# Attention stage of a hybrid decoder layer: turning the values inside the steps

## The chip, the cores and the metric

The kernel runs on one core of a Trainium2 chip. The metric is the device time of one execution in microseconds (us), as the median of three runs. Beside it stands one execution recorded by the hardware profiler, from which all rows below come.

## The reference

One layer: RMS norm, one wide input projection, three token mixers (a chunked state-space scan, a dilated sliding-window attention, a short gated convolution), each projected and merged with gates, an output projection, a norm and the residual. The change is in the attention. For each of 8 heads and three patterns (window, dilation) = (128, 1), (512, 4), (2048, 16), a query looks at 128 earlier keys that lie `dilation` apart, and at itself:

```
def dilated_window_attention(q, k, v, window, dilation):
    ...
    kb = key_blocks(k)
    vb = key_blocks(v)
    ...
    scores = jnp.einsum("brnqhd,brnkhd->brnhqk", qb, kb) * (ATTN_HEAD_DIM ** -0.5)
    scores = jnp.where(valid[None, None, :, None], scores, -jnp.inf)
    m = jnp.max(scores, axis=-1, keepdims=True)
    p = jnp.exp(scores - m)
    den = jnp.sum(p, axis=-1)
    o = jnp.einsum("brnhqk,brnkhd->brnqhd", p, vb) / jnp.moveaxis(den, -1, -2)[..., None]
```

The sequence has 2048 positions, a head has 64 channels, and all is float32. Keys and values are shared by the three patterns; each pattern has its own queries.

## The kernel before, in words

The kernel runs five stages one after the other: projection, scan with gates, attention, merge of the branches, output. `attention_stage` (from line 961) is a program for each engine inside one block, and each engine's program has a loop over four pairs of heads (`PAIRS`, slots 0 and 1 of a pair). Nothing orders the engines but semaphores, and each engine and each DMA queue works in the order written.

The values of a pair come from memory with the channels on the partitions (`v_t`, in the trace a_v) and are needed with the positions on the partitions (`v_tok`, a_vt). TensorE turns them, 12 quarters (`NV`), four for each pattern g, each quarter four transposes of 128 x 128 (L1137) into one of four buffers of `ps_t` (a_pst). VectorE copies the even turns out (L1037), ScalarE the odd ones (L1196, the line of its copy). Before the change all 12 quarters stand at the head of the loop over the pairs, ahead of the first score.

Then come 48 steps (`NS`), index j: slot 0 with patterns 0, 1 and 2, eight steps each (`SPAN`), then slot 1 likewise. A step treats two blocks of 128 queries. Its parts:

- score(j), TensorE, L1155: queries against the high and the low part of the keys (`k_hi`, `k_lo`; strided by the dilation), into `ps_s`. It waits for mask j-2.
- mask, VectorE, L1238: scale, mask and row maximum.
- exp(j), ScalarE, L1207.
- turn(j-2), TensorE, L1165: transposes the probabilities into `ps_t`; the evacuation (L1026 to L1030 on VectorE, L1196 on ScalarE) copies them to `probs_t`. The turns of values and of probabilities share one numbering n, by which the buffer (n % 4) and the copying engine (n % 2) are chosen; before, n is 12 + j for the probabilities.
- output(j-4), TensorE, L1179: probabilities times values, 65 columns; VectorE copies four blocks at a time to `att` (L1249).

The keys of a slot are loaded raw by SP (`load_k`, L1060, two loads of 512 KB), split by ScalarE (`split_hi`, L1047) and POOL (`split_lo`, L1051). ScalarE does the split for slot 1 at j = 10 and the one for the next pair's slot 0 at j = 34, between exp(j) and the copy that belongs to step j.

SP's order within a pair (from L1090) is: wait until `v_turned` says that this pair's 12 quarters are turned, load the next pair's values (L1092), load the keys of slot 1 (L1060), the three queries of slot 1 (L1066), the keys of the next pair, its queries and the stores of `att` (L1075, L1080):

```
sp.wait_ge(v_turned, NV * i + NV)
sp.dma_start(v_t[:], d["kv"][bass.ds(4 + following, 1)].rearrange("o p t -> p (o t)")
             ).then_inc(v_loaded, 16)
load_k(i, 1, 2 * i + 1)
```

Of the kernel before, what the change touches and what calls it, by code (L numbers as in the profile page):

```python
# [21 lines left out]
P = 128  # L22
# [5 lines left out]
HEADS, HDIM, GROUPS, STATE = 16, 64, 4, 128  # L28
# [6 lines left out]
OUT_W = HDIM + 1  # L35
# [925 lines left out]
def attention_stage(nc, w, d, ident, raw, y_lo):  # L961
# [11 lines left out]
    blocks = [[(r, n) for r in range(x) for n in range(SEQ // x // P)] for x in dil]  # L973
    steps = [(g, sl, b) for sl in range(2) for g in range(3) for b in range(0, NB, 2)]
    NS, NV = len(steps), 12
    SPAN = NB // 2
    TURNS = (NS + NV) // 2
    stores = [1, dil[1], 1]
    with ExitStack() as stack:
        s = Scope(nc, stack)  # L980
        q_s = s.sb("a_q", [P, 3, SEQ], F32R)
        k_raw, v_t = s.sb("a_kraw", [P, SEQ]), s.sb("a_v", [P, SEQ])
# [30 lines left out]
        def strided(ap, g):  # L1013
            return ap.rearrange("p (m r) -> p r m", r=dil[g])
# [4 lines left out]
        def evacuate(eng, parity, copy, i, j):  # L1019

            eng.wait_ge(p_turned, NS * i + j + 5)
            eng.wait_ge(o_made, NS * i + j + 1)
            n = NV + j
            g, sl, b = steps[j]
            if width(g, b) == width(g, b + 1) == 2 * P:
                copy(probs_t[:, j % 4], ps_t[:, n % 4]).then_inc(t_taken[parity], 1)  # L1026
            elif width(g, b + 1) == P:
                copy(probs_t[:, j % 4, 1::2], ps_t[:, n % 4, 1::2]).then_inc(t_taken[parity], 1)
            else:
                copy(probs_t[:, j % 4, 1:], ps_t[:, n % 4, 1:]).then_inc(t_taken[parity], 1)  # L1030

        def evacuate_v(eng, parity, copy, i):

            eng.wait_ge(o_made, NS * i + 4)
            for n in range(parity, NV, 2):
                eng.wait_ge(v_turned, NV * i + n + 1)
                copy(v_tok[:, n // 4, n % 4 * 4:n % 4 * 4 + 4].rearrange("p b (s q) -> p b s q", q=OUT_W)[:, :, :, :HDIM],  # L1037
                     ps_t[:, n % 4].rearrange("p b (s q) -> p b s q", q=HDIM)).then_inc(t_taken[parity], 1)

        def scored(unit, g):  # L1040

# [2 lines left out]
        def split_hi(act, unit, sl):  # L1044
            act.wait_ge(k_loaded, 32 * unit + 32)
            act.wait_ge(s_made, NS + NS // 2 * (unit - 1))
            act.activation(k_hi[:, sl], k_raw[:], ACT.Copy).then_inc(k_hi_made, 1)  # L1047
# [5 lines left out]
        with nc.Block() as block:  # L1053
# [70 lines left out]
            @block.tensor  # L1124
            def _(pe):
                pe.sem_inc(s_made, NS)
                pe.sem_inc(p_turned, 4)
                pe.sem_inc(o_made, 4)
                pe.wait_ge(ones_made, 1)
                with pe.Fori(0, PAIRS) as i:  # L1130
                    pe.wait_ge(v_loaded, 16 * i + 16)
                    for n in range(NV):
                        g = n // 4
                        pe.wait_ge(t_taken[n % 2], TURNS * i + n // 2 + 1)
                        for b in range(4):
                            r, m = blocks[g][n % 4 * 4 + b]
                            last = pe.transpose(ps_t[:, n % 4, b], strided(v_t[:], g)[:, r, m * P:(m + 1) * P], ident[:])  # L1137
                        last.then_inc(v_turned, 1)

                    def score(j):  # L1140
                        g, sl, b = steps[j]
                        if b == 0:
                            pe.wait_ge(q_loaded[g], 32 * i + 16 * sl + 16)
                            if g == 0:
                                pe.wait_ge(k_made, 2 * i + sl + 2)
                        pe.wait_ge(masked, NS * i + j + 1)
                        bank = ps_s[:, j % 2].rearrange("p e k -> p (e k)")
                        for e in range(2):

                            at = (b + e) * P  # L1150
                            r, m = blocks[g][b + e]
                            n = width(g, b + e)
                            for k, first in ((k_hi, True), (k_lo, False)):
                                keys = strided(k[:, sl], g)[:, r, (m + 1) * P - n:(m + 1) * P]
                                last = pe.matmul(bank[:, (e + 1) * 2 * P - n:(e + 1) * 2 * P], q_s[:, g, at:at + P], keys,  # L1155
                                                 start=first, stop=not first)
                        last.then_inc(s_made, 1)

                    def turn(j):
                        g, sl, b = steps[j]  # L1160
                        pe.wait_ge(exped, NS * i + j + 5)
                        pe.wait_ge(t_taken[j % 2], TURNS * i + (NV + j) // 2 + 1)
                        for e in range(2):
                            for h in range(2 - width(g, b + e) // P, 2):
                                last = pe.transpose(ps_t[:, (NV + j) % 4, 2 * e + h], probs[:, j % 4, e, h * P:(h + 1) * P],  # L1165
                                                    ident[:])
                        last.then_inc(p_turned, 1)

                    def output(j):
                        g, sl, b = steps[j]  # L1170
                        if j == 0:
                            pe.wait_ge(t_taken[1], TURNS * i + NV // 2 + 2)
                        pe.wait_ge(t_taken[j % 2], TURNS * i + (NV + j) // 2 + 3)
                        if j % 2 == 0:
                            pe.wait_ge(o_taken, 24 * i + j // 2 + 1)
                        for e in range(2):
                            first = 2 - width(g, b + e) // P
                            for h in range(first, 2):
                                last = pe.matmul(ps_o[:, j // 2 % 2, (b + e) % 4, :OUT_W], probs_t[:, j % 4, 2 * e + h],  # L1179
                                                 v_tok[:, g, b + e - 1 + h, sl * OUT_W:(sl + 1) * OUT_W],  # L1180
                                                 start=h == first, stop=h == 1)
                        last.then_inc(o_made, 1)

                    for j in range(NS + 4):
                        if j < NS:
                            score(j)
                        if 2 <= j < NS + 2:
                            turn(j - 2)
                        if j >= 4:
                            output(j - 4)  # L1190

            @block.scalar
            def _(act):
                act.sem_inc(exped, 4)
                act.sem_inc(t_taken[1], 2)
                copy = lambda to, of: act.activation(to, of, ACT.Copy)  # L1196
                split_hi(act, 0, 0)
                with act.Fori(0, PAIRS) as i:
                    evacuate_v(act, 1, copy, i)
                    for j in range(NS + 2):  # L1200
                        if j < NS:
                            g, sl, b = steps[j]
                            act.wait_ge(masked, NS * i + j + 3)
                            act.wait_ge(p_turned, NS * i + j + 1)
                            for e in range(2):
                                n = width(g, b + e)
                                last = act.activation(probs[:, j % 4, e, 2 * P - n:], scores[:, j % 4, e, 2 * P - n:],  # L1207
                                                      ACT.Exp, bias=att[:, g, b + e, 2 * OUT_W + sl:2 * OUT_W + sl + 1],
                                                      scale=-1.0)
                            last.then_inc(exped, 1)  # L1210

                            if j % (NS // 2) == SPAN + 2:
                                sl = j // (NS // 2)
                                split_hi(act, 2 * i + sl + 1, 1 - sl)
                        if j >= 2 and j % 2:
                            evacuate(act, 1, copy, i, j - 2)

            @block.vector
            def _(dve):
# [4 lines left out]
                    dve.sem_inc(stored[g], 16 * stores[g])  # L1224
                dve.wait_ge(band_turn, 3)
                keys = band[:].rearrange("p a k -> p (a k)")
                with dve.Fori(0, PAIRS) as i:
                    evacuate_v(dve, 0, dve.tensor_copy, i)
                    for j in range(NS + 5):
                        if j < NS:  # L1230
                            g, sl, b = steps[j]
# [8 lines left out]
                                    in1=keys[:, 2 * P - n:], scale=-HDIM ** -0.5, scalar=-NEG, op0=ALU.add, op1=ALU.min,  # L1240
                                    accum_out=att[:, g, b + e, 2 * OUT_W + sl:2 * OUT_W + sl + 1])
                            last.then_inc(masked, 1)
                        if 2 <= j < NS + 2 and j % 2 == 0:
                            evacuate(dve, 0, dve.tensor_copy, i, j - 2)
                        if j >= 6 and j % 2 == 0:
                            grp = j // 2 - 3
# [639 lines left out]
```

## Time and profile before

| | us |
|---|---|
| median of three runs | 3264.48 (3257.29 to 3268.20) |
| profiled execution, own time | 3256.7 |
| its span, first to last instruction | 3255.0 |
| TensorE busy | 3087.3 (95%) |
| VectorE, ScalarE, POOL busy | 1072.2, 859.7, 750.5 |
| attention stage, first transpose to last output | 2257.2 to 2628.6 |

The page of the profile gives the busy time of each engine as a share of the span; the trace itself can be asked for stretches, for what each engine waited for, and for the instructions in order of time. PE is TensorE, PEld its weight loads, DVE VectorE, ACT ScalarE, SP the engine that issues loads. A name such as `a_pst<-ident,a_v` is the tile written and the tiles read. "[6.34 <-DVE a_vt L1037]" is idle time before an instruction and what ended it; "issue" stands where the profile shows nothing that was waited for.

### The profile page before, as it was taken

To read this page: it belongs to the slowest core of one execution; us is meant where nothing else is said; L and a number is where in the kernel's file an instruction comes from. 1 tells how busy PE (TensorE), PEld (TensorE's weight loads), DVE (VectorE), ACT (ScalarE), POOL (GpSimd) and SP (SyncE) were. 2 spreads that over 40 slices of the span, in tenths; PEclk is the share of its full clock that TensorE was granted. 3 is DMA by queue.
4 is the path that set the end of the run, shared out by engine and by line. 5 is a ranking of instruction groups with operands and counts; after the bars stand their busy time and mean duration, and the time that the engine had idled before them with its cause. 6 is when DMAs were issued, how large, how long until landed. Compare 5 with 4: busy or idle time off the path is not lost. (4 is left out here: it accounts for less than half of the span.)

```text
span 3255.0 us, 42118 instructions
## 1 busy us (share of the span) xinstructions
PE 3087.3 (95%) x15420; PEld 2598.0 (80%) x15420; DVE 1072.2 (33%) x1821; ACT 859.7 (26%) x1459; POOL 750.5 (23%) x406
## 2 busy tenths in 40 slices
PE   6999999999999999999999999998899968989798
PEld 5888888888888888888887888887898856778687
DVE  6003434201000011110002544544565567762333
ACT  5110000000000000000113455554566642332232
POOL 7111111111111111112233353451111034421000
PEclk9999999999999999999999999999999989999999
DMA  5121222334421210112324344444544457775543
GB/s 156 61 74 64 75 73 77 87 113 129 116 71 64 77 35 23 39 39 92 97 91 130 106 129 111 117 132 163 149 121 139 143 179 234 237 243 143 173 137 116
DMA packets 333307, 370.78 MB, mean 114 GB/s; under 512 B 22832, under 2 KB 283952, under 8 KB 319664
## 3 DMA queue, kind: packets, MB, share of 16 engines
q1 hardware_dynamic: 314864, 270.51, 28.7%
q10 hardware_dynamic: 16080, 91.23, 8.1%
q0 software_dynamic: 2304, 8.39, 0.7%
q8 instruction: 20, 0.33, 0.0%
q14 instruction: 39, 0.32, 0.0%
HBM read 234.43 MB, written 135.66 MB: 114 GB/s over the span
## 5 line engine op out<-in xcount | busy, mean ns | idle before, releaser
L281 PE MATMUL p_acc<-h,w_hi 128*128 128x512 f32 x2464 | 968.9, 393 | 3.5 <-DVE h L482 3.4
L283 PE MATMUL p_acc<-h,w_lo 128*128 128x512 f32 x2464 | 964.7, 392 | 0.0
L282 PE MATMUL p_acc<-h,w_hi 128*128 128x512 f32 x2464 | 958.8, 389 | 0.0
L283 PEld LDWEIGHTS p_acc<-h,w_lo 128*128 128x128 f32 x2464 | 462.7, 188 | 104.5
L282 PEld LDWEIGHTS p_acc<-h,w_hi 128*128 128x128 f32 x2464 | 462.9, 188 | 101.3
L281 PEld LDWEIGHTS p_acc<-h,w_hi 128*128 128x128 f32 x2464 | 463.1, 188 | 99.8 <-DVE h L482 4.8
L242 POOL CAST w_hi<-raw 128x1024 fp32r<-128x1024 f32 x88 | 91.6, 1041 | 1349.9 <-PE p_acc L283 1344.5
L1556 PE MATMUL b_acc<-b_yhi,b_whi 128*128 128x512 f32 x512 | 206.0, 402 | 44.5 <-DVE b_ylo_ssd L1647 26.5
L244 POOL TENSOR_TENSOR w_lo<-raw,w_hi 128x1024 fp32r<-128x1024 f32 x88 | 212.1, 2410 | 7.0
L379 ACT ACTIVATE p_stage<-p_acc 128x1024 f32<-128x1024 f32 (+1 forms) x45 | 64.2, 1427 | 554.0 <-PE p_acc L283 554.0
L1558 PE MATMUL b_acc<-b_yhi,b_wlo 128*128 128x512 f32 x512 | 203.1, 397 | 0.0
L1207 ACT ACTIVATE a_probs<-a_scores,a_att 128x256 f32<-128x256 f32 (+1 forms) x384 | 155.6, 454 | 101.2 <-DVE a_att L1238 99.0
L509 DVE TENSOR_SCALAR work<-p_acc,p_cw,p_cb 128x2048 f32<-128x2048 f32 x16 | 38.6, 2410 | 383.9 <-PE p_acc L283 383.9
L1238 DVE CUSTOM_DVE_ANT_0 a_scores<-a_pss,a_band 128x256 f32<-128x256 f32 (+1 forms) x384 | 125.1, 363 | 115.9 <-PE a_pss L1155 113.4
L765 PE MATMUL s_acc<-h,w_hi 128*128 128x512 f32 x384 | 162.5, 423 | 0.0
L1179 PE MATMUL a_pso<-a_vt,a_probst 128*128 128x65 f32 x1200 | 156.1, 269 | 0.0
L1556 PEld LDWEIGHTS b_acc<-b_yhi,b_whi 128*128 128x128 f32 x512 | 98.7, 193 | 70.3 <-issue 36.1
L767 PE MATMUL s_acc<-h,w_lo 128*128 128x512 f32 x384 | 150.4, 392 | 0.0
L1179 PEld LDWEIGHTS a_pso<-a_vt,a_probst 128*128 128x128 f32 x1200 | 149.8, 193 | 0.3
L766 PE MATMUL s_acc<-h,w_hi 128*128 128x512 f32 x384 | 149.7, 390 | 0.0
L535 DVE TENSOR_TENSOR work<-p_acc,work 128x2048 f32<-128x2048 f32 x4 | 9.2, 2293 | 417.4 <-PE p_acc L283 417.4
L1432 POOL TENSOR_TENSOR b_wlo<-b_raw,b_whi 128x2048 fp32r<-128x2048 f32 (+2 forms) x20 | 82.1, 4103 | 231.1 <-ACT b_whi L1466 231.1
(196 smaller groups left out, 4208.2 us busy)
## 6 DMA issues: line engine op xcount, KB each, us to landing
raw<-w_in SPq DMA_DIRECT2D x113, 512.0 KB, 4.2
a_q<-s_qs SPq DMA_DIRECT2D x27, 1024.0 KB, 5.7
b_gate<-s_gates SPq DMA_DIRECT2D x48, 512.0 KB, 7.1
s_xbc<-p_stage ACTq DMA_DIRECT2D x16, 1024.0 KB, 3.9
work<-s_xbc SPq DMA_DIRECT2D x16, 1024.0 KB, 6.9
b_att<-s_att SPq DMA_DIRECT2D x24, 528.0 KB, 5.7
s_qs<-p_stage ACTq DMA_DIRECT2D x24, 512.0 KB, 5.5
s_qs<-work ACTq DMA_DIRECT2D x24, 512.0 KB, 8.2
```

The costliest lines, as they stand in the source:

```text
L244: pool.tensor_tensor(w_lo[:, slot], raw[:, slot], w_hi[:, slot], ALU.subtract).then_inc(w_made[slot], 1)
L281: pe.matmul(to, w_hi[:, slot, c], h_hi, start=c == 0, stop=False)
L282: pe.matmul(to, w_hi[:, slot, c], h_lo, start=False, stop=False)
L283: last = pe.matmul(to, w_lo[:, slot, c], h_hi, start=False, stop=c == KC - 1)
L765: pe.matmul(acc_tiled, w_hi[:, slot, b], hi, start=b == 0, stop=False)
L766: pe.matmul(acc_tiled, w_hi[:, slot, b], lo, start=False, stop=False)
L767: last = pe.matmul(acc_tiled, w_lo[:, slot, b], hi, start=False, stop=b == KC - 1)
L1179: last = pe.matmul(ps_o[:, j // 2 % 2, (b + e) % 4, :OUT_W], probs_t[:, j % 4, 2 * e + h], v_tok[:, g, b + e - 1 + h, sl * OUT_W:(sl + 1) ...
L1207: last = act.activation(probs[:, j % 4, e, 2 * P - n:], scores[:, j % 4, e, 2 * P - n:], ACT.Exp, bias=att[:, g, b + e, 2 * OUT_W + sl:2 * ...
L1238: last = dve.tensor_tensor_reduce(out=scores[:, j % 4, e, 2 * P - n:], in0=ps_s[:, j % 2, e, 2 * P - n:], in1=keys[:, 2 * P - n:], scale=- ...
L1556: pe.matmul(to, w_hi[:, k, c], y_hi[:, c, span], start=c == at, stop=False)
L1558: last = pe.matmul(to, w_lo[:, k, c], y_hi[:, c, span], start=False, stop=c == at + n - 1)
```

## The change

Each pair now turns its own patterns 1 and 2 and the next pair's pattern 0 within its steps: the quarters of pattern 1 at steps 0 to 3, of pattern 2 at steps 8 to 11, and of pattern 0, from the values of the next pair, at steps 36 to 39. In each of these steps TensorE turns the quarter between score(j) and turn(j-2). Pair 0's pattern 0 is turned ahead of the loop; the last pair turns four quarters that nobody uses. The numbering of turns is now made from a list of both kinds in order (`turns`, `turn_of`), starting at 4. The engine that copies a probability turn follows from it and is another one for steps 0 to 9. Waits are added so that the outputs of a pattern come after its values, and values are overwritten only when the outputs that read them are done. SP's program has not been edited.

```diff
+    FIRST = NV // 3
...
+    v_at = {at + n: (g, n) for g, at in ((1, 0), (2, SPAN), (0, 4 * SPAN + 4)) for n in range(NV // 3)}
+    turns = [x for j in range(NS + 4) for x in ([("v", *v_at[j])] if j in v_at else []) + (
+        [("p", j - 2)] if 2 <= j < NS + 2 else [])]
+    turn_of = {x: FIRST + n for n, x in enumerate(turns)}
...
+        def evacuate_v(eng, parity, copy, i, j):
+
+            g, quarter = v_at[j]
+            done = FIRST + list(v_at).index(j) + 1
+            eng.wait_ge(o_made, NS * i + {0: 4 * SPAN + 4, 1: 1, 2: 4}[g])
+            eng.wait_ge(v_turned, NV * i + done)
+            take_v(parity, copy, g, quarter, turn_of["v", g, quarter])
...
+                pe.wait_ge(v_loaded, 16)
+                for n in range(FIRST):
+                    pe.wait_ge(t_taken[n % 2], n // 2 + 1)
+                    turn_values(0, n, n)
                 with pe.Fori(0, PAIRS) as i:
-                    pe.wait_ge(v_loaded, 16 * i + 16)
-                    for n in range(NV):
-                        g = n // 4
+                    def turn_v(j):
+                        g, quarter = v_at[j]
+                        n = turn_of["v", g, quarter]
+                        if g == 0 and quarter == 0:
+                            pe.wait_ge(v_loaded, 16 * i + 32)
                         pe.wait_ge(t_taken[n % 2], TURNS * i + n // 2 + 1)
...
                     def output(j):
                         g, sl, b = steps[j]
+                        n = turn_of["p", j]
+                        if sl == 0 and b == 0 and g > 0:
+                            for quarter in (2, 3):
+                                v = turn_of["v", g, quarter]
+                                pe.wait_ge(t_taken[v % 2], TURNS * i + v // 2 + 3)
...
                         if j < NS:
                             score(j)
+                        if j in v_at:
+                            turn_v(j)
                         if 2 <= j < NS + 2:
                             turn(j - 2)
...
                 split_hi(act, 0, 0)
+                evacuate_first_v(act, 1, copy)
                 with act.Fori(0, PAIRS) as i:
-                    evacuate_v(act, 1, copy, i)
...
-                        if j >= 2 and j % 2:
+                        if j in v_at and turn_of["v", *v_at[j]] % 2:
+                            evacuate_v(act, 1, copy, i, j)
+                        if j >= 2 and turn_of["p", j - 2] % 2:
                             evacuate(act, 1, copy, i, j - 2)
...
+                evacuate_first_v(dve, 0, dve.tensor_copy)
                 with dve.Fori(0, PAIRS) as i:
-                    evacuate_v(dve, 0, dve.tensor_copy, i)
...
-                        if 2 <= j < NS + 2 and j % 2 == 0:
+                        if j in v_at and turn_of["v", *v_at[j]] % 2 == 0:
+                            evacuate_v(dve, 0, dve.tensor_copy, i, j)
+                        if 2 <= j < NS + 2 and turn_of["p", j - 2] % 2 == 0:
                             evacuate(dve, 0, dve.tensor_copy, i, j - 2)
```

## Rows read from the trace of the kernel before

**Rows 1.** The page: busy us and share of the span of each engine.

```profile
PE 3087.3 (95%) x15420; PEld 2598.0 (80%) x15420; DVE 1072.2 (33%) x1821; ACT 859.7 (26%) x1459; POOL 750.5 (23%) x406
```

**Rows 2.** Stretch of pair 1: us; busy PE, PEld, DVE, ACT, POOL; PEclk, DMA, GB/s.

```profile
2365.00:2443.00 78.00, 77.07 (x637) 74.69 (x635) 50.19 (x239) 52.46 (x123) 9.11 (x2) 1.00 0.45 133
```

**Rows 3.** Timeline from pair 0 to pair 1 (start, duration, engine, line, what).

```profile
2351.43 1.92 PE L1137 MATMUL a_pst<-ident,a_v 128*128 128x128 f32 x16
2351.70 1.28 ACT L1196 ACT_TABLE_LOAD   x1 [1.07 <-PE a_pso L1179]
2352.23 0.71 SPq L1080 DMA_DIRECT2D s_att<-a_att  x1
...
2358.94 1.29 DVE L1037 COPY a_vt<-a_pst 128x512 f32<-128x512 f32 x2 [6.88 <-issue]
2359.69 5.56 PE L1137 MATMUL a_pst<-ident,a_v 128*128 128x128 f32 x32 [6.34 <-DVE a_vt L1037]
...
2365.01 0.31 PE L1155 MATMUL a_pss<-a_khi,a_q 128*128 128x128 f32 x1
2365.51 0.37 SPq L1092 DMA_DIRECT2D a_v<-s_kv  x1
2365.91 0.29 DVE L1238 CUSTOM_DVE_ANT_0 a_scores<-a_pss,a_band 128x128 f32<-128x128 f32 x1 [0.39 <-PE a_pss L1155]
2366.18 1.18 SPq L1060 DMA_DIRECT2D a_kraw<-s_kv  x2
```

**Rows 4.** Waits of the attention stage (who for whom: total us, times, longest).

```profile
DVE a_vt L1037 <- issue: 20.1, 3, 6.9
```

**Rows 5.** Timeline, head of pair 0.

```profile
2256.67 4.52 POOL L1051 TENSOR_TENSOR a_klo<-a_kraw,a_khi 128x2048 fp32r<-128x2048 f32 x1 [8.20 <-ACT a_khi L1047]
2257.17 7.54 PE L1137 MATMUL a_pst<-ident,a_v 128*128 128x128 f32 x48 [14.76 <-DMA a_v<-s_kv]
...
2264.47 0.31 PE L1155 MATMUL a_pss<-a_khi,a_q 128*128 128x128 f32 x1
...
2265.36 0.29 DVE L1238 CUSTOM_DVE_ANT_0 a_scores<-a_pss,a_band 128x128 f32<-128x128 f32 x1 [0.37 <-PE a_pss L1155]
```

**Rows 6.** Timeline, first steps of pair 1: exp(0) to exp(2), output(0), score(6).

```profile
2366.67 2.59 ACT L1207 ACTIVATE a_probs<-a_scores,a_att 128x128 f32<-128x128 f32 x6 [0.79 <-DVE a_att L1238]
...
2369.88 0.78 PE L1179 MATMUL a_pso<-a_vt,a_probst 128*128 128x65 f32 x6
...
2372.28 0.36 PE L1155 MATMUL a_pss<-a_khi,a_q 128*128 128x256 f32 x1
```

**Rows 7.** Groups by line, attention stage: ScalarE's copy of a value quarter.

```profile
L1196 ACT ACTIVATE a_vt<-a_pst 128x512 f32<-128x512 f32 x24 | 14.0, 597 | 31.5 <-PE a_pst L1137 31.5
```

**Rows 8.** Timeline and one stretch, pair 0, steps 10 to 13: split of keys, turn(11).

```profile
2289.08 1.91 ACT L1047 ACTIVATE a_khi<-a_kraw 128x2048 fp32r<-128x2048 f32 x1 [6.88 <-DMA a_kraw<-s_kv]
...
2291.84 1.12 PE L1165 MATMUL a_pst<-ident,a_probs 128*128 128x128 f32 x4 [5.25 <-ACT a_probs L1207]
```

```profile
2294.00:2296.00 2.00, 2.00 (x11) 1.99 (x11) 0.27 (x3) 0.24 (x1) 1.60 (x1) 0.50 0.04 8
```

**Rows 9.** Timeline, pair 1: score(11), split, turn(9), output(7); then pair 1's end.

```profile
2382.05 0.46 PE L1155 MATMUL a_pss<-a_khi,a_q 128*128 128x256 f32 x1
...
2382.64 1.90 ACT L1047 ACTIVATE a_khi<-a_kraw 128x2048 fp32r<-128x2048 f32 x1
...
2383.02 0.62 PE L1165 MATMUL a_pst<-ident,a_probs 128*128 128x128 f32 x4
...
2383.48 1.00 PE L1179 MATMUL a_pso<-a_vt,a_probst 128*128 128x65 f32 x8
...
2443.97 1.92 PE L1137 MATMUL a_pst<-ident,a_v 128*128 128x128 f32 x16
```

**Rows 10.** Key loads L1060, from issue to landing: pair 1, then pair 0.

```profile
DMA to landing us min/median/max: 7.3/8.2/9.0
...
DMA to landing us min/median/max: 12.7/13.6/14.6
```

More of the change, by code:

```diff
@@ L1022, in evacuate @@
             eng.wait_ge(o_made, NS * i + j + 1)
-            n = NV + j
+            n = turn_of["p", j]
             g, sl, b = steps[j]
@@ L1030, in evacuate, with take_v, evacuate_first_v @@
                 copy(probs_t[:, j % 4, 1:], ps_t[:, n % 4, 1:]).then_inc(t_taken[parity], 1)
[L1032 to L1038, printed above, removed]
+        def take_v(parity, copy, g, quarter, n):
+            copy(v_tok[:, g, quarter * 4:quarter * 4 + 4].rearrange("p b (s q) -> p b s q", q=OUT_W)[:, :, :, :HDIM],
+                 ps_t[:, n % 4].rearrange("p b (s q) -> p b s q", q=HDIM)).then_inc(t_taken[parity], 1)
+        def evacuate_first_v(eng, parity, copy):
+            for n in range(parity, FIRST, 2):
+                eng.wait_ge(v_turned, n + 1)
+                take_v(parity, copy, 0, n, n)
+        def evacuate_v(eng, parity, copy, i, j):
[4 more added lines that the diff above has]
+            take_v(parity, copy, g, quarter, turn_of["v", g, quarter])
         def scored(unit, g):
@@ L1129, in _, with turn_values @@
                 pe.wait_ge(ones_made, 1)
-                with pe.Fori(0, PAIRS) as i:
-                    pe.wait_ge(v_loaded, 16 * i + 16)
-                    for n in range(NV):
-                        g = n // 4
+                def turn_values(g, quarter, n):
+                    for b in range(4):
+                        r, m = blocks[g][quarter * 4 + b]
+                        last = pe.transpose(ps_t[:, n % 4, b], strided(v_t[:], g)[:, r, m * P:(m + 1) * P], ident[:])
+                    last.then_inc(v_turned, 1)
+                pe.wait_ge(v_loaded, 16)
+                for n in range(FIRST):
+                    pe.wait_ge(t_taken[n % 2], n // 2 + 1)
+                    turn_values(0, n, n)
+                with pe.Fori(0, PAIRS) as i:
+                    def turn_v(j):
[3 more added lines that the diff above has]
+                            pe.wait_ge(v_loaded, 16 * i + 32)
                         pe.wait_ge(t_taken[n % 2], TURNS * i + n // 2 + 1)
[L1135 to L1138, printed above, removed]
+                        turn_values(g, quarter, n)
                     def score(j):
@@ L1160, in turn @@
                         g, sl, b = steps[j]
+                        n = turn_of["p", j]
                         pe.wait_ge(exped, NS * i + j + 5)
-                        pe.wait_ge(t_taken[j % 2], TURNS * i + (NV + j) // 2 + 1)
+                        pe.wait_ge(t_taken[n % 2], TURNS * i + n // 2 + 1)
                         for e in range(2):
                             for h in range(2 - width(g, b + e) // P, 2):
-                                last = pe.transpose(ps_t[:, (NV + j) % 4, 2 * e + h], probs[:, j % 4, e, h * P:(h + 1) * P],
+                                last = pe.transpose(ps_t[:, n % 4, 2 * e + h], probs[:, j % 4, e, h * P:(h + 1) * P],
                                                     ident[:])
@@ L1170, in output @@
                         g, sl, b = steps[j]
+                        n = turn_of["p", j]
+                        if sl == 0 and b == 0 and g > 0:
+                            for quarter in (2, 3):
+                                v = turn_of["v", g, quarter]
+                                pe.wait_ge(t_taken[v % 2], TURNS * i + v // 2 + 3)
                         if j == 0:
-                            pe.wait_ge(t_taken[1], TURNS * i + NV // 2 + 2)
-                        pe.wait_ge(t_taken[j % 2], TURNS * i + (NV + j) // 2 + 3)
+                            for quarter in (2, 3):
+                                v = turn_of["v", 0, quarter] - len(turns)
+                                pe.wait_ge(t_taken[v % 2], TURNS * i + max(v // 2 + 3, 4))
+                        pe.wait_ge(t_taken[n % 2], TURNS * i + n // 2 + 3)
                         if j % 2 == 0:
```

## The prediction

> **What bounds the kernel now.** I read the busy shares of the page, then the table of stretches, then the timeline of the attention stage and its waits. TensorE is busy 95% of the span [rows 1], and within a pair of the attention stage 77.07 of 78 us at clock 1.00 [rows 2]: the 48 steps of a pair are bound by TensorE's own stream, and anything put into them costs its full length. Between two pairs it is different. Behind the last output of pair 0 TensorE turns four quarters of the values (16 transposes from 2351.43, 1.92 us), then is idle 6.34 us until VectorE takes the first of them, and turns the other eight in 5.56 us; score(0) starts at 2365.01 and the first mask at 2365.91 [rows 3]. VectorE's own idle time there is not a wait for TensorE: it is charged to "issue", 3 times, 20.1 us in all [rows 4], once at each return to the top of the loop over the pairs. The chain that counts is therefore the one through VectorE's return, 6.88 us of idle time and then the values, before any score can be masked.
>
> **Part 1, between pairs.** After the change the first VectorE work of a pair is mask(0), not a copy of values, and score(0) and score(1) need no VectorE at all. If VectorE still comes back at 2358.94, mask(0) starts there and not at 2365.91: 6.97 us earlier [rows 3]. There are three such places: -20.9 us. The quarters of pattern 1 at steps 0 and 1 lie under VectorE's idle time and cost nothing; without that cover they would cost 0.46 us each.
>
> What does the return cost? The row shows idle time and no cause. The Trainium skill ("Runtime: NRT & Kernel Launch", Instruction fetch mechanics) states that a taken branch whose target lies outside the small fetched window stops the engine until the target page has come by DMA. By that rule the 6.88 us stay whatever work comes first in the loop, which is what the sum above has; were they bound to the value copies they would go too (rival 2). ScalarE and TensorE start their first work of the new pair within about a microsecond, ScalarE at 2351.70 [rows 3], which the rule alone does not explain.
>
> **Part 2, head of pair 0.** All twelve quarters run ahead of score(0) now, 2257.17 to 2264.47, mask(0) at 2265.36. With four quarters left there, the key's low half becomes the last to arrive: it starts at 2256.67 and takes 4.52 us, 2261.19 [rows 5]. Score(0) follows, the mask 0.9 us later as now: 2262.1, or -3.3 us.
>
> **Part 3, refilling the steps.** From mask(0) the chain to the first output takes 3.97 us now and score(6) starts at 6.37 us [rows 3, 6]. ScalarE gets more in it: the table load, now done at 2351.70 ahead of the value copies [rows 3] while nobody waits, comes in front of the first Exp, because that is the first activation of the loop's body (1.28 us); one value copy of 0.60 us [rows 7]; and the turned probabilities of step 0, which VectorE copies now, because the numbering of turns shifts (0.6 us, taken from the same row). ScalarE is thereby 2.5 us late. TensorE has no slack left for the two quarters at steps 2 and 3, and starts from the lower clock after its idle time. Counted from the start of mask(0), ScalarE's order is: mask done 0.8, table 2.1, exp(0) 2.9, exp(1) 3.8 (six Exps take 2.59 us [rows 6], so a step 0.9), value copy 4.4, exp(2) 5.3, copy of probabilities 0 5.9, exp(3) 6.8, copy 1 7.4. Output(0) can start at 5.9, output(1) at 7.4, and with 1.0 us for it score(6) at 8.4: 2.0 later than now. With the lower clock, at which turns and outputs take about twice as long, as behind the idle time in [rows 8], it comes at about 10: 3.6 later. I take 3.0: four pairs, +12 us (8 to 14.4).
>
> The Trainium skill ("ScalarE activation tables: per-element evaluation and per-set limits", Table sets in the compiler and the runtime) says that the table loads are placed block by block. By it the load goes in front of the first Exp in the body; were it placed ahead of the loop, this term would be about 5 us smaller in all. The row has it inside the loop.
>
> **Part 4, quarters inside full steps.** Eight quarters a pair go into steps 8 to 11 and 36 to 39. Four transposes take TensorE from 2383.02 to 2383.48, 0.46 us [rows 9]. 8 x 0.46 = 3.7 us a pair, on the bound itself: +14.7 us. VectorE and ScalarE have room for the copies. In all, 52 quarters are turned instead of 48.
>
> **Part 5, the queue of loads.** This decides. SP waits for all twelve turns of the pair before it reloads a_v, and behind that a_v load in the same queue stand the two loads of the keys of the second slot. Now the twelfth turn comes before step 0. Afterwards it is the turn in step 11. ScalarE, however, asks for these keys in step 10 (split_hi), ahead of the copy of turned probabilities 8 and of exp(11). There is no deadlock, since TensorE reaches turn 11 without them, but then everything stops.
>
> Time from t, the start of score(11). Turn 11 starts at t+0.97 (2382.05 to 2383.02 [rows 9]) and ends at t+1.6. SP issues a_v 0.26 us after the last transpose (2359.69+5.56 to 2365.51), the first key load 0.67 us later and the second 0.6 after that [rows 3]: t+3.2. The second lands 9.0 us after issue [rows 10]: t+12.2. The split takes 1.90 [rows 9], then ScalarE copies probabilities 8, 0.6: t+14.7. Only then output(8) can start. TensorE would have been there at t+2.7 (step 11 with its quarter) plus a score and a turn, 1.4: t+4.1. It idles 10.6 us.
>
> The profile already holds this stall, once. In pair 0 the key loads are issued into a full queue and land after 14.6 us [rows 10]; ScalarE waits 6.88 us for them, TensorE is idle 5.25 us, and works on at granted clock 0.50 [rows 8]. What it costs: pair 0 runs 2264.47 to 2351.43, 86.96 us, pair 1 runs 2365.01 to 2443.97, 78.96 us [rows 3, 5, 9]: 8.0 us, idle 5.25 plus 2.75 for the lower clock (1.2 instead of 2.4 GHz) and the restart. In the same way the new stall costs 10.6 + 2.75 = 13.3 us in each of four pairs, and replaces the one of pair 0: 4 x 13.3 - 8.0 = +45.2 us. Bounds: 12 us a pair if the restart is cheaper (+40), 15.5 if it is dearer (+54), and 5.6 us more if pair 0 lands as late as it does now (14.6 for 9.0).
>
> The query loads behind it in the queue are wanted from step 24 on, more than 20 us later; a_v for the next pair at step 36. Neither is late.
>
> **Sum.** -20.9 - 3.3 + 12 + 14.7 + 45.2 = +47.7 us. On the profiled execution (3256.7 us, span 3255.0) this is 3304; the median of the timed runs, 3264.5, lies 7.8 above it and gives 3312. I take 3310.
>
> **Rivals.**
> 1. The keys are not late, so the stall is missing: the queue would have to let them past a_v, or turn 12 be counted earlier. It decides from a landing at t+1.6 (t+4.1 less 0.6 and 1.90); they would have to land 10.6 us earlier than worked out. Then pair 0's stall goes as well: -20.9 - 3.3 + 12 + 14.7 - 8.0 = -5.5, 3259, no difference that can be told. For it: the first keys in each pair are never waited for in pairs 1 to 3, where the split starts without idle time [rows 9]. Against it: the order in SP's queue and the counts, which are fixed. 5%.
> 2. VectorE's idle time at the loop's top goes with the value copies. Then 3 x 6.6 us or so more are gained: 47.7 - 20 = +28, 3292. For it: ScalarE and TensorE show no such stop. Against it: it is charged to no engine and no DMA, and the work before and after the branch is unchanged in kind, as is the store issued at 2352.23, beside which it falls [rows 3]. The skill's rule on fetching, above, speaks against this rival too. 8%.
> 3. The stall is there and much dearer: the lower clock holds through the following steps, or the key loads meet other traffic in every pair and land after 14.6 us, 5.6 more each: +70, 3334. Against it: in pairs 1 to 3 they land within 9.0. 5%.
> 4. Both 1 and 2: -25, 3239. 2%.
>
> **How the numbers follow.** Forecast 80%, rivals 5, 8, 5 and 2. The forecast's own bounds: below, 3256.7 - 24.2 + 8 + 14.7 + 40 = 3295; above, 3264.5 - 24.2 + 14.4 + 14.7 + 54 + 5.6 = 3329. The range takes in rival 2's time: 3290 to 3328. A measurement of this kernel tells 0.3%, some 10 us. Slower by more than that: forecast and rivals 2 and 3, 93%; within it: rival 1, 5%; faster: rival 4, 2%.
>
> **What would show it.** ScalarE idle before the split of the keys about 11 us in each pair, released by the key load, four times; a_v issued some 30 us after the pair's first score and not 0.5; TensorE idle some 10 us once a pair, in step 12, with clock 0.50 behind it. Between pairs TensorE ahead by two scores and two quarters, VectorE still idle 6 to 7 us, then mask(0) directly; the table load in front of the first Exp. From the score(0) of pair 0 to that of pair 1, 100.5 us now with a stall of its own [rows 3, 5], it becomes about 105.5, and the same in the pairs behind it. The forecast is wrong if ScalarE's wait is short, or if the stop of VectorE is gone.

## The result, and the profile after

The changed kernel takes 3325.4 us (median; 3305.4 to 3334.4), the kernel before 3265.8 us: ratio 1.0175, interval 1.0129 to 1.0222, slower by 1.75%. Each is the median of four executions. The profiled execution takes 3305.4 us (span 3303.7) against 3256.7, so 48.7 us more. The runs of the changed kernel lie further apart than those of the kernel before; the reason is a finding of its own, below.

The waits of the attention stage after the change (who for whom: total us, times, longest):

```profile
ACT a_khi L1064 <- DMA a_kraw<-s_kv: 47.0, 4, 11.9
PEld a_pso L1213 <- issue: 43.3, 4, 11.0
PE a_pso L1213 <- ACT a_probst L1232: 42.3, 4, 10.8
DVE a_scores L1276 <- issue: 21.9, 3, 7.5
```

ScalarE waits for the keys of slot 1 four times, 11.75 us on average, and TensorE four times for ScalarE's copy of the turned probabilities, 42.3 us in all. VectorE's idle time at the loop's return is still there, 21.9 us for 20.1 [rows 4].

The timeline of one such stall, in pair 1 (the answer to [rows 8, 9]):

```profile
2388.69 0.37 SPq L1109 DMA_DIRECT2D a_v<-s_kv  x1
...
2389.36 1.18 SPq L1077 DMA_DIRECT2D a_kraw<-s_kv  x2
...
2398.59 1.91 ACT L1064 ACTIVATE a_khi<-a_kraw 128x2048 fp32r<-128x2048 f32 x1 [11.52 <-DMA a_kraw<-s_kv]
2400.41 0.47 ACT L1232 ACTIVATE a_probst<-a_pst 128x384 f32<-128x384 f32 x1
...
2401.11 1.54 PE L1213 MATMUL a_pso<-a_vt,a_probst 128*128 128x65 f32 x6 [10.35 <-ACT a_probst L1232]
```

SP issues a_v at the twelfth turn, 30.5 us after the pair's first score, and not 0.5 us after it as in [rows 3]; the keys land behind it, are split, and the small copy at 2400.41 releases output(8).

The return from pair 0 to pair 1 (the answer to [rows 3]):

```profile
2358.18 0.32 PE L1181 MATMUL a_pss<-a_khi,a_q 128*128 128x128 f32 x1
...
2359.72 0.65 PE L1150 MATMUL a_pst<-ident,a_v 128*128 128x128 f32 x4
2366.21 0.29 DVE L1276 CUSTOM_DVE_ANT_0 a_scores<-a_pss,a_band 128x128 f32<-128x128 f32 x1 [7.38 <-issue]
...
2366.95 1.28 ACT L1243 ACT_TABLE_LOAD   x1 [9.55 <-DVE a_att L1276]
...
2375.70 0.36 PE L1181 MATMUL a_pss<-a_khi,a_q 128*128 128x256 f32 x1
```

TensorE is two scores and two quarters ahead when VectorE comes back, mask(0) is its first work, the table load stands in front of the first Exp, and score(6) starts at 2375.70.

### The profile page after: what moved, and what is told of

The parts are those of the page before. It is cut to its first block and busy times, and to the rows that moved or that the text cites. A ratio compares the mean times of both kernels' runs of the same rounds, so it can differ in the third digit from the quotient of the medians.

```text
span 3303.7 us, 42164 instructions
## 1 busy us (share of the span) xinstructions
PE 3100.0 (94%) x15436; PEld 2613.6 (79%) x15436; DVE 1069.8 (32%) x1823; ACT 856.3 (26%) x1461; POOL 751.5 (23%) x406
## 5 line engine op out<-in xcount | busy, mean ns | idle before, releaser
L1213 PE MATMUL a_pso<-a_vt,a_probst 128*128 128x65 f32 x1200 | 163.0, 276 | 42.3 <-ACT a_probst L1232 42.3
L1213 PEld LDWEIGHTS a_pso<-a_vt,a_probst 128*128 128x128 f32 x1200 | 156.5, 201 | 43.5 <-issue 43.3
L1181 PE MATMUL a_pss<-a_khi,a_q 128*128 128x256 f32 (+1 forms) x384 | 129.7, 360 | 20.0 <-DVE a_att L1276 19.4
```

## Experiments

**The late keys, taken away.** Only SP's order is edited:

```diff
+                    load_k(i, 1, 2 * i + 1)
                     sp.wait_ge(v_turned, NV * i + NV)
                     sp.dma_start(v_t[:], ...).then_inc(v_loaded, 16)
-                    load_k(i, 1, 2 * i + 1)
```

> The changed kernel with one edit in SP's order: the two key loads of slot 1 stand ahead of the wait for the turned values and of the a_v load. Theory (the late keys cost 45 us): ScalarE's wait before the split at step 10 is gone in pairs 1 to 3 and at most 3 us in pair 0, where the queue is full of block loads; TensorE's idle 10.5 us in step 12 and the lower clock behind it are gone; time 3250 to 3268, within 0.3% of the kernel before. Rival (the quarters inside the steps and the refill carry most of the loss): at least 3290.

3253.5 us, 12 runs from 3248 to 3257; ratio to the kernel before 0.9976 (0.9963 to 0.9989). The profiled span is 3253.3, 50.4 us under that of the changed kernel. The place of the two key loads in SP's order carries the whole loss. What is left of ScalarE's wait is 2.2 us in pair 0; TensorE is idle 1.0 us for it and then works at clock 0.50 from 2288 to 2295. The rival of the record, that quarters and refill carry the loss, is out.

**The late keys alone, given to the kernel before.**

```diff
                     following = (i + 1) % PAIRS
+                    sp.wait_ge(s_made, NS * i + NS + 12)
                     sp.wait_ge(v_turned, NV * i + NV)
```

> The kernel before with one added wait in SP: a_v and, behind it, the keys of slot 1 are loaded only when score(11) is done; nothing else is changed. Theory: this alone brings the stall, 13.3 us in each of four pairs less the 8.0 us that pair 0 has already, about +45 us: 3300 to 3320, ScalarE waiting 10 to 12 us for the keys four times. If the restart at the lower clock is what spreads the runs of the changed kernel (3305 to 3334), these runs spread by 15 us or more too. Rival: the stall hides behind the two steps that TensorE is ahead, under +25 us.

3320.8 us (3311.6 to 3323.3), ratio 1.0175 (1.0149 to 1.0200): the loss of the change as first measured, with nothing of its turning. It is 61 us over the kernel before beside it (3259.4), dearer than the +45 of the expectation and just above its range; the five runs spread by 11.7 us, not by the 15 expected. ScalarE's four waits are 45.2 us, 11.3 on average, as expected. The granted clock tells why. Two of its four stalls in stretches (us; busy PE, PEld, DVE, ACT, POOL; PEclk; DMA share; GB/s), first pair 0, then pair 3:

```profile
2292.00:2296.00 4.00, 1.51 (x8) 1.51 (x8) 0.00 (x0) 4.00 (x8) 2.29 (x1) 0.50 0.30 123
2296.00:2300.00 4.00, 4.00 (x20) 3.99 (x20) 1.45 (x6) 1.69 (x5) 2.25 (x1) 0.50 0.01 4
2300.00:2304.00 4.00, 4.00 (x32) 3.98 (x33) 1.70 (x10) 1.77 (x5) 0.00 (x0) 0.86 0.36 123
2304.00:2308.00 4.00, 4.00 (x39) 4.00 (x38) 2.51 (x15) 2.19 (x7) 0.00 (x0) 1.00 0.34 141
```

```profile
2622.00:2626.00 4.00, 4.00 (x22) 3.99 (x20) 1.01 (x5) 1.83 (x6) 2.87 (x1) 0.50 0.00 0
2634.00:2638.00 4.00, 4.00 (x22) 4.00 (x20) 1.08 (x9) 1.39 (x4) 0.00 (x0) 0.50 0.00 0
2646.00:2650.00 4.00, 4.00 (x21) 4.00 (x22) 1.70 (x10) 1.56 (x6) 0.00 (x0) 0.50 0.09 16
2650.00:2654.00 4.00, 4.00 (x26) 4.00 (x26) 2.09 (x10) 1.21 (x4) 0.00 (x0) 0.67 0.99 338
```

In pair 0 the clock is back at its upper level 6 to 7 us after TensorE resumes (the next expectation, on the spread, puts this at 12 us, which is too long). In pair 3 it stays at 0.50 for some 32 us, although TensorE is busy all of the 4 us of every stretch. From one a_v load to the next, the stalls with the short restart (pairs 0 and 1) make it 104.8 and 105.8 us, the long restart of pair 2 makes it 116.2, where the kernel before takes 92.2 (2365.51 [rows 3] to 2457.72): a stall costs 12.6 to 13.6 us with the short restart and 24 us with the long one.

**The spread.** The changed kernel again.

> The changed kernel once more, for the spread of its runs (3305 to 3334, where the kernel before has 3252 to 3271). In before_late the granted clock came back about 12 us after the stall in two pairs and about 36 us after it in the two others, which were 10 us longer. Theory: each of the four stalls ends in the short or in the long restart, so the runs lie near 3305 + 10 n with n from 0 to 4, and the mean clock falls by 0.003 with each. Rival: the spread comes from elsewhere; then time and mean clock of the runs do not go together so.

Its six runs are 3304.0, 3318.1, 3331.7, 3332.7, 3345.3 and 3345.7 us with mean clocks 0.975, 0.970, 0.964, 0.965, 0.960 and 0.960. Time and clock go together, in steps of 14 us and 0.005. The picture holds, the step was expected at 10 us. Against the kernel before beside them the ratio is 1.0234 (1.0205 to 1.0263), more than the 1.0175 of the first four; the median of all ten executions is 3331.9 us. The profiled executions of the changed kernel (spans 3303.7 and 3302.4 us) are both of the cheap end; a long restart of this kernel is thus seen in times and mean clocks only, and in stretches only in before_late and, behind a shorter idle time, in kf_table. The kernel before does the same on a smaller scale: of the 24 runs beside keys_first, 14 lie at 3252 to 3261 with clock 0.980 to 0.982 and ten at 3265 to 3271 with 0.976 to 0.978.

**The stall of the kernel before.** SP's load of the merge stage's first block is moved behind the keys of slot 1 of pair 0, and nothing else.

```diff
-                load_first_block(sp, w, d, raw, y_lo, next_loaded)
...
                     load_k(i, 1, 2 * i + 1)
+                    if first:
+                        load_first_block(sp, w, d, raw, y_lo, next_loaded)
```

> The kernel before with one thing moved: SP loads the first block of the merge stage after the keys of slot 1 of pair 0, not ahead of the loop. Theory: the stall of pair 0 (8.0 us in the profiled execution) goes, and with it the long restarts that put a third of the runs of the kernel before near 3268 and not 3257; the runs lie together at 3246 to 3254. Rival: the stall is another's and stays; or the block loads, now during the first steps, delay the queries of slot 1 and take it back.

Eight runs, all from 3248.5 to 3252.7; ratio 0.9962 (0.9948 to 0.9976) to a kernel before whose 13 runs lay at 3252.6 to 3269.5. In its trace pair 0's steps take 78.95 us (2264.44 to 2343.39), where they took 86.96 [rows 3, 5]: both the 8 us and the second cluster belong to the one stall of pair 0.

**The price of a quarter.** In keys_first each quarter from step 8 on is turned twice.

```diff
-                        turn_values(g, quarter, n)
+                        turn_values(g, quarter, n, 2 if j >= SPAN else 1)
```

> keys_first with each value quarter at steps 8 to 11 and 36 to 39 turned twice into the same buffer: 128 more transposes. Theory (these steps are bound by TensorE): each of the 32 added quarters costs its 0.46 us, +14.7 us over keys_first. Rival (they fill gaps of TensorE): under +4 us.

3263.3 us, 9.7 us over keys_first and not 14.7. By pairs (from one a_v load to the next) it is 95.82 for 92.58 us and 95.70 for 92.13 in pairs 1 and 2: 3.2 and 3.6 us for eight quarters, 0.43 us each, near the 0.46 worked out. From pair 0 to pair 1 it is 96.18 for 95.97: there the added work gives the keys time. ScalarE's wait falls from 2.2 to 0.9 us and the clock does not fall behind it. The theory holds; the total misses because the extra work hides a small stall.

**VectorE's return.** In keys_first the query load and the store of pattern 2 are held until the next pair's second mask.

```diff
+                    if not first:
+                        sp.wait_ge(masked, NS * i + 4)
+                        load_q(i, 0, 2 * i, 2)
+                        store(i - 1, 2)
                     load_k(i, 1, 2 * i + 1)
```

> keys_first, and the load of the pattern 2 queries and the store of pattern 2, which SP issues just as VectorE comes back to the top of the loop, are held until the second mask of the next pair is done. Theory A (VectorE's idle time at the return is a fetch of its instructions that queues behind these two transfers): its idle time falls from 7.4 to 2 us or less, three times, 14 to 17 us faster than keys_first. Theory B (the return costs this by itself, whatever is in flight): 7 us as before and the time of keys_first within 4 us.

3240.8 us, ratio 0.9937 (0.9914 to 0.9959), 12.8 us under keys_first. The waits of keys_first and of kf_late_store:

```profile
DVE a_scores L1276 <- issue: 20.8, 3, 7.4
```

```profile
DVE a_scores L1286 <- issue: 9.4, 3, 3.2
```

The idle time is 3.1 us each for 6.9. Theory A holds in kind, but neither number was met: some 3 us stay, and the gain is 12.8 us and not 14 to 17. The added wait also holds the two key loads of slot 1 behind it, which keys_first issues at 2351.42, within VectorE's return. They are held in the next two runs as well, so they make no difference between these. Which of the two is it, the query load or the store? Each was held alone, the other put back in its old place (only one of the two added lines kept).

> kf_late_store with the load of the pattern 2 queries back in its old place: only the store of pattern 2 is held until VectorE has returned. If the store is what delays the return (528 KB in small packets, issued 0.2 us after VectorE's last copy), its idle time is 3 to 4 us as in kf_late_store and the time within 3 us of it. If the queries' load does it, 6 to 7 us and the time of keys_first. Each a part: between.

> kf_late_store with the store of pattern 2 back in its old place: only the load of the pattern 2 queries is held until VectorE has returned. kf_store_only had 6.2 us of idle time at each return against 3.1 with both held. If the queries' load alone delays the return, 3 to 3.5 us here and the time of kf_late_store (3241). If either transfer in flight is enough, 5 to 6.5 us and about 3250.

With the store alone held, 3249.9 us, and this wait:

```profile
DVE a_scores L1285 <- issue: 18.6, 3, 6.3
```

With the queries' load alone held, 3242.7 us, and this one:

```profile
DVE a_scores L1285 <- issue: 9.3, 3, 3.1
```

So it is mostly the load of the queries, 1 MB issued about 3 us before the return, and not the store, which I had pointed at: 6.2 us against 3.1. The store and the key loads together account for the 0.7 us between kf_store_only and keys_first.

That the idle time is a fetch can be read from the traces, in the packets of the DMA queue that the profile calls "instruction". In each of the three returns of before, keys_first, kf_late_store, kf_store_only and kf_q_only, the last such packet stands 2.0 to 2.5 us before VectorE's first operation. What the runs change is when it comes: 4.2 us after VectorE's last copy in keys_first (2349.96, packet at 2354.14, mask(0) at 2356.49), 3.7 us in kf_store_only, and 0.7 us in kf_late_store and in kf_q_only (2351.00, 2351.69, 2354.12). The stretches 2354 to 2355 of keys_first and 2351 to 2352 of kf_q_only have one each (packets, MB, share of the 16 engines):

```profile
q14 instruction: 1, 0.01, 1.9%
```

```profile
q14 instruction: 1, 0.01, 3.3%
```

The Trainium skill ("Runtime: NRT & Kernel Launch", Instruction fetch mechanics) states that a taken branch whose target is not in the current window forces a DMA fetch of the target page before execution goes on. The traces agree: VectorE's idle time ends 2.0 to 2.5 us behind the packet, and with the queries' load in flight the packet comes 3 us or more later. The queue's rows do not name the engine for which a packet comes; that it is VectorE's goes by the times, the same in all fifteen returns.

**The table load.** In keys_first, and then in kf_late_store, a tiny Exp at the head of ScalarE's loop body draws the table load away from the first mask.

```diff
                 with act.Fori(0, PAIRS) as i:
+                    act.activation(tiny[:, 0:1], zero[:, 0, 0:1], ACT.Exp)
```

> keys_first with one tiny Exp (one column) at the head of ScalarE's loop body, ahead of every wait, so that the table load runs while VectorE is still away. Theory (ScalarE is the chain of the refill): 1.28 us less in each of four pairs, 3 to 6 us faster than keys_first. Rival (the refill is held by VectorE or by TensorE at the lower clock): within 1.5 us.

> kf_late_store and the tiny Exp of kf_table together. If the two gains are of different chains they add: 3 to 6 us faster than kf_late_store, about 3236, 0.7% faster than the kernel before. If the shorter return leaves the table load in the shadow of something else: within 1.5 us of kf_late_store.

3253.0 us against 3253.5, so nothing that can be told: the rival holds. The table load does leave the chain, to 8.7 us ahead of mask(0), but score(6) comes only 0.2 to 0.4 us earlier behind mask(0) (9.23 and 9.11 us for 9.67 and 9.31 in keys_first). TensorE works at the lower clock just then. What that costs the refill kf_late_store shows: behind its second return the clock stays at 1.00 and score(6) comes 8.03 us after mask(0), behind the first, at 0.50 from 2352.9 on, 9.52 us. With the shorter return of kf_late_store it is 3238.7 against 3240.8, 2.1 us, between the two expectations and inside the spread. The run kf_table also shows how little it takes to bring the clock down. TensorE's only wait in pair 0 from 2270 to 2300, and then three stretches with the columns as above:

```profile
PE a_pso L1214 <- ACT a_probst L1234: 2.0, 1, 2.0
```

```profile
2286.00:2288.00 2.00, 0.14 (x2) 0.00 (x0) 1.45 (x6) 2.00 (x3) 0.41 (x1) 1.00 0.97 410
2290.00:2292.00 2.00, 2.00 (x12) 2.00 (x10) 0.78 (x4) 0.89 (x3) 2.00 (x1) 0.50 0.35 139
2320.00:2322.00 2.00, 2.00 (x11) 2.00 (x11) 1.18 (x5) 0.80 (x2) 0.00 (x0) 0.50 1.03 410
```

After an idle stretch of 2 us the clock went to 0.50 at about 2289 and came back at about 2323, and TensorE was fully busy in between. It does not always fall: behind an idle stretch of 2.3 us in kf_late_store (2436.4 to 2438.7) it stays at 1.00. Its two dear runs, 3268.7 and 3269.3 us, have clock 0.979, the other ten 0.981 to 0.983.

**All together.** kf_all, with the block loads behind the keys of pair 0, as in before_block.

> kf_all with the block loads of the merge stage moved behind the keys of slot 1 of pair 0. Theory: ScalarE's 3.6 us wait in pair 0 and the low clock behind it go; the runs at 3250 to 3254 disappear, all lie at 3232 to 3240, about 0.75% under the kernel before. Rival: the block loads collide with other loads of pair 0 and the gain is under 1 us.

3234.1 us, six runs from 3231.9 to 3236.2; ratio 0.9909 (0.9892 to 0.9926), to a kernel before whose median beside it was 3265.5 us, with more dear runs than in the other two lots; against their 3259 it is 0.8% faster. It beats both kernels, and the dear runs are gone. Its stalls for the keys are gone from all four pairs: the wait that is left is the one for the very first keys, ahead of the loop:

```profile
ACT a_khi L1065 <- DMA a_kraw<-s_kv: 11.0, 1, 11.0
```

## Why the prediction was right

The forecast was 3310 us, range 3290 to 3328; the profiled execution was worked out at 3304 and took 3305.4, the median of four executions 3325.4. That this median lies within the range is in part luck: six of the ten executions of this kernel lie above 3328, and their median, 3331.9 us, is nearer to the 3334 of rival 3. The mechanism was right, the size of one term was not. By its own terms:

- **The queue of loads (+45.2): right in place and mechanism.** TensorE's idle time was put at 4 x 10.6 = 42.4 us and is 42.3. The last key load lands 9.0 us after issue in the record and 8.5 to 8.9 after the change. keys_first takes the loss away, before_late brings it alone.
- **The restart (2.75 us in each stall): right in the profiled execution, too small for the median.** It was read from one restart in the only stall of the trace [rows 8]. From one a_v load to the next the changed kernel takes 107.4, 106.2 and 105.2 us, for the 105.5 forecast. Runs have both kinds, the long one 10 to 14 us dearer. The step that failed is "In the same way the new stall costs 10.6 + 2.75 = 13.3 us in each of four pairs": that term has a tail, and its mean over runs is higher by about 5.6 us (counted from the steps in the times, ten executions have 16 long restarts in 40 stalls, at 14 us each). Median less profiled execution, 3325.4 - 3305.4 = 20 us, is this tail; the forecast had 7.8 us for it, taken over from the kernel before, whose tail has one stall and not four. Rival 3 named a lower clock that holds through the following steps, at 5%; going by the times, eight of the ten runs have it behind at least one stall.
- **Between pairs (-6.97 each): nearly.** From the end of the pair's outputs to mask(0) it was 14.48 us (2351.43 to 2365.91 [rows 3]) and is 8.03 (2358.18 to 2366.21): -6.45. VectorE's idle time stayed, 7.38 for 6.88, so rival 2 is out as a forecast. But the idle time can be had, by moving a load and not the value copies.
- **Head of pair 0 (-3.3).** First transpose to mask(0): 8.19 us [rows 5], now 5.62 (2253.78 to 2259.40): -2.6. Score(0) waits for the key's low half, as said; the mask comes 1.4 us behind it, since the clock is low.
- **Refill (+3.0 each).** Mask(0) to score(6): 6.37 us [rows 3, 6], now 9.49 (2366.21 to 2375.70): +3.1. That ScalarE is its chain is only half right: kf_table takes the 1.28 us of the table load out of the chain, and score(6) comes 0.2 to 0.4 us earlier.
- **Quarters in full steps (0.46 each).** Step 11 took 2.24 us and takes 2.69 (2386.82 to 2389.51): 0.45.

Without the stall the rest of the sum was -5.5 us; keys_first gives -5.8 between the medians measured together (3253.5 for 3259.4). So close a match is luck in part: without its ten dear runs the kernel before has 3257.2, which makes it -3.7, the spans of the profiled executions differ by 1.7 us (3253.3 for 3255.0), and keys_first keeps a small stall in pair 0 that the sum puts at nothing. What holds is rival 1's statement: with the keys in time, no difference from the kernel before beyond 0.3%.

## What to carry to other kernels

A wait in a queue orders everything behind it. When a step is moved later, look for each queue that waits for that step, and ask of every transfer behind the wait who needs it first; here moving the two key loads in SP's program turns +1.75% into -0.24%. A stall that shows once in a trace is a price for its mechanism, but take the price of the clock's recovery as a range, and time enough runs to see its tail. Idle time at a loop's return can depend on transfers in flight just then: hold back those which nobody needs yet.

## What the runs showed of the hardware

The granted clock can fall to 0.50 (1.2 GHz of 2.4) even behind an idle stretch of TensorE of 1.0 or 2.0 us (keys_first, kf_table), and can stay at 1.00 behind one of 2.3 us (kf_late_store). It comes back 4 to 11 us after TensorE resumes or 32 to 36 us after it, and both within one program and at the same steps (before_late). What decides between the two was not found: the stretches show TensorE fully busy in both. VectorE's return to the top of a long loop costs 3.1 us with the queries' load held and 6.2 to 7.4 us with this 1 MB load in flight, and its first operation follows 2.0 to 2.5 us behind a packet of the instruction queue; ScalarE and TensorE show no such stop here, and why was left open.
